# Sampled attention regrouped: one group of plain matrix products per sequence in place of two

## The chip, the cores and the metric

The kernel runs on one core of one Trainium2 chip. The metric is device time in microseconds. A profiled execution gives a trace of each engine: PE is TensorE's matrix product, PEld its weight load, DVE VectorE, ACT ScalarE, POOL GpSimd and SPq the queue of SyncE from which the loads and stores are issued.

## What is computed

One step of a one-layer decoder trunk: a prompt of 1,024 rows and 8 sampled sequences of 8 rows each go through a projection, two branches (a recurrent one, mLSTM, and windowed attention with a sink), a gated merge, an output product and an MLP. The change touches the attention of the sampled sequences alone. Each of them reads its own 128 cached keys and values and the new rows:

```python
def swa_sample(q, k, v, ck, cv, sinks):
    kk = jnp.concatenate([ck.astype(k.dtype), k], axis=1)
    vv = jnp.concatenate([cv.astype(v.dtype), v], axis=1)
    ...
    qh = q.reshape(B, T, A_KV, A_GROUP, A_HD).transpose(0, 2, 3, 1, 4)
    o = sink_attend(qh, kk.transpose(0, 2, 1, 3), vv.transpose(0, 2, 1, 3), mask, sinks)
```

`sink_attend` is a softmax over scaled, masked scores with one more logit per head in the denominator, and then the product with the values.

## The kernel before

Each engine runs a program of its own, in order, and the programs meet at semaphores. The large products (projection, output product, MLP) split each float32 operand into a high and a low part and add three products of the fp32r type. In the projection such a piece of work is a *unit*: 24 products into one bank, of 384 columns (two in three) or 320 columns (one in three), issued by `proj_unit` (line 889). The small products of the attention are plain float32 products and transposes (line 845, by `tr`; lines 1097, 1098 and 1118).

The attention does not run by itself. Lists made at the top of the file (`FILL_P0`, `FILL_SS`, `FILL_P1`, from `spread`) say which units stand between its steps, and `fill` is called with them in every engine's program. `attention()` on PE runs `prompt(0)`, `sampled`, `prompt(1)`. `FILL_SS` has 17 entries: entry 0 holds three units, each of the entries 1 to 16 one. ACT reads each unit (a tanh, line 1451), and DVE applies the gate (lines 2100 to 2104). A unit with number 0 of a block makes SP load the next block of weights (`load_block`, four transfers of 256 KB here, behind a wait for all units of the block two back); in `FILL_SS` these are, besides the first unit, the entries 4, 10 and 16.

For a sampled sequence b the steps are, on PE: `ss_keys(b)` transposes the cached keys (two transposes, waits for their load), `ss_scores(b)` (16 products on 64 x 32 tiles of the array), `ss_transposes(b)` of the probabilities, `ss_values(b)` (16 products with the cached and the new values, on 128 x 32 and 64 x 32 tiles), `ss_outputs(b)` (one transpose of the gathered output). Between them ACT copies (`ss_keys`, `ss_pT`, `ss_out`) and takes exponents (`ss_exps`), and DVE masks (`ss_mask`), divides (`ss_divide`, last line 2038) and gathers (`ss_gather`, line 2050). Cached keys and values have two buffers each. In SP's program `load_keys(s)` waits until the keys of sequence s-2 are transposed (`sk_t`), and `load_values(s)` until the values of sequence s-2 are used (`ss_v`):

```python
if s >= 2:
    sp.wait_ge(sk_t, s - 1)
...
if s >= 2:
    sp.wait_ge(ss_v, s - 1)
```

In the kernel before, PE's round b is: keys of b+1, one unit, outputs of b-1, transposes of b, scores of b+1, one unit, values of b. So each sequence has two groups of plain products between units: (values b-1, keys b+1) and (outputs b-1, transposes b, scores b+1).

After the last round `prompt(1)` begins: scores of its first two heads' units, the last `ss_outputs`, one unit of fill, and `at_transposes`, which waits for DVE's `at_mask` (lines 1991 to 2003) and `at_divide` (line 2011).

Of the kernel before, what the change touches and what calls it, by code (L numbers as in the profile page):

```python
# [38 lines left out]
NSEQ = 8  # L39
# [188 lines left out]
HALF = 2 * NB  # L228
# [18 lines left out]
def layer_kernel(nc, x_prompt, x_sample, state_C, state_n, state_m, cache_k, cache_v, norm_attn, w_in, b_gate,  # L247
# [20 lines left out]
    with ctx:  # L268
# [61 lines left out]
        s = ExitStack()  # L330
# [264 lines left out]
        def _(sp):  # L595
# [154 lines left out]
            def sampled(fills):  # L750
                def load_keys(s):
                    if s >= 2:
                        sp.wait_ge(sk_t, s - 1)
                    sp.dma_start(kc[:, s % 2, :], cache_k[0, s].rearrange("w h d -> w (h d)")).then_inc(kc_in[s % 2], 16)

                def load_values(s):
                    if s >= 2:
                        sp.wait_ge(ss_v, s - 1)
                    sp.dma_start(vc[:, s % 2, :], cache_v[0, s].rearrange("w h d -> w (h d)")).then_inc(vc_in[s % 2], 16)

                sp.wait_ge(at_v, NB)
                sp.wait_ge(at_p1, HALF)
                load_keys(0)
                load_keys(1)
                load_values(0)
                fill(fills[0])
                for s in range(1, NSEQ):
                    fill(fills[2 * s - 1])
                    if s + 1 < NSEQ:
                        load_keys(s + 1)  # L770
                    fill(fills[2 * s])
                    load_values(s)
                fill(fills[2 * NSEQ - 1])
                fill(fills[2 * NSEQ])
                sp.wait_ge(ko_e, 2)
                sp.dma_start(p_k[0, 0].rearrange("t h d -> t (h d)"), kout[:, 0, :]).then_inc(out_dma, 16)
                sp.dma_start(p_v[0, 0].rearrange("t h d -> t (h d)"), avn[:, NT - 2, :]).then_inc(out_dma, 16)
                for s in range(NSEQ):
                    at = slice(s * DSEQ, (s + 1) * DSEQ)
                    sp.dma_start(s_k[0, s, WIN - DSEQ:].rearrange("t h d -> t (h d)"),  # L780
                                 kout[at, 1, :]).then_inc(out_dma, 16)
                    sp.dma_start(s_v[0, s, WIN - DSEQ:].rearrange("t h d -> t (h d)"),
                                 avn[at, NT - 1, :]).then_inc(out_dma, 16)
# [59 lines left out]
        def _(pe):  # L843
# [283 lines left out]
            def prompt(p, fills):  # L1127

                pe.wait_ge(free_a, ATT_FIRST + (ATT_UNITS[0] + ATT_UNITS[1] if p else 0))
                if p:  # L1130
                    pe.wait_ge(ss_te, NSEQ)
                u0 = p * HALF
                at_scores(u0)
                at_scores(u0 + 1)
                if p:
                    ss_outputs(NSEQ - 1)
                fill(fills[0])
                for n in range(0, HALF, 2):
                    u = u0 + n
                    at_transposes(u)  # L1140
                    if n:
                        at_values(u // 2 - 1)
                    if n + 2 < HALF:
                        at_scores(u + 2)
                        at_scores(u + 3)
                    at_transposes(u + 1)
                    fill(fills[n + 1])
                    fill(fills[n + 2])
                at_values(u // 2)

            def sampled(fills):

                for x, i in enumerate((NT - 2, NT - 1)):
                    for p in range(2):
                        last = tr(bank[5 + x][0:rows_of(i), p * P:(p + 1) * P], akT[:, p, cols(i)], P)
                    last.then_inc(ko_t, 1)
                fill(fills[0])
                pe.wait_ge(free_a, FIRST_UNIT[17])
                pe.wait_ge(at_o, NB)
                ss_keys(0)  # L1160
                ss_scores(0)
                pe.wait_ge(ko_e, 2)
                for b in range(NSEQ):
                    if b + 1 < NSEQ:
                        ss_keys(b + 1)
                    fill(fills[2 * b + 1])
                    if b >= 1:
                        ss_outputs(b - 1)
                    ss_transposes(b)
                    if b + 1 < NSEQ:  # L1170
                        ss_scores(b + 1)
                    fill(fills[2 * b + 2])
                    ss_values(b)

            def attention():
                pe.wait_ge(ml_te, 2 * S_PER)
# [196 lines left out]
        def _(act):  # L1373
# [230 lines left out]

            def prompt_act(p, fills):
                u0 = p * HALF
                if p:
                    ss_out(NSEQ - 1)
                at_exps(u0)
                at_exps(u0 + 1)  # L1610
                fill(fills[0])
                for n in range(0, HALF, 2):
                    u = u0 + n
                    at_copy(u)
                    if n:
                        at_out(u // 2 - 1)
                    at_copy(u + 1)
                    if n + 2 < HALF:
                        at_exps(u + 2)
                    fill(fills[n + 1])  # L1620
                    if n + 2 < HALF:
                        at_exps(u + 3)
                    fill(fills[n + 2])
                at_out(u // 2)

            def sampled_act(fills):
                act.wait_ge(ko_t, 2)
                nc.scalar.activation(kout[:, 0, :], bank[5][:, 0:256], ACT.Copy).then_inc(ko_e, 1)
                nc.scalar.activation(kout[0:64, 1, :], bank[6][0:64, 0:256], ACT.Copy).then_inc(ko_e, 1)
                fill(fills[0])  # L1630
                ss_keys(0)
                ss_exps(0)
                for b in range(NSEQ):
                    if b + 1 < NSEQ:
                        ss_keys(b + 1)
                    fill(fills[2 * b + 1])
                    if b >= 1:
                        ss_out(b - 1)
                    ss_pT(b)
                    if b + 1 < NSEQ:  # L1640
                        ss_exps(b + 1)
                    fill(fills[2 * b + 2])


            def square_x(i):
# [136 lines left out]
        def _(dve):  # L1782
# [193 lines left out]
            def at_mask(u):  # L1976
                i, p, gg = at_unit(u)
                dve.wait_ge(at_s, u + 1)
                if u == 0:
                    dve.wait_ge(consts, 5)  # L1980
                if u == HALF:
                    dve.wait_ge(ss_v, NSEQ)
                    dve.wait_ge(ss_ot, NSEQ)
                st = ast[:, u % 2]
                later = amask[:, :].bitcast(I32).unsqueeze(1).broadcast_to([P, 2, P])

                def part(half, kb):
                    return score_bank(u, half)[:, :].rearrange("q (g b k) -> q g b k", g=2, b=2)[:, :, kb, :]
                for half in range(2):
                    prev = part(half, 0) if i else nbig[:, :].unsqueeze(2).broadcast_to([P, 2, P])  # L1990
                    ins = nc.vector.copy_predicated(part(half, 1), later, prev)
                link(ins)
                for half in range(2):
                    ins = nc.vector.tensor_reduce(st[:, 0, 2 * half:2 * half + 2], part(half, 1), mybir.AxisListType.X,
                                                  ALU.max)
                link(ins)
                sk = sink_b[:, :].rearrange("t (v g) -> t v g", g=GRP)[:, 2 * p:2 * p + 2, 2 * gg:2 * gg + 2]

                def by_half(x):
                    return st[:, x, :].rearrange("t (v g) -> t v g", g=2)  # L2000
                link(nc.vector.scalar_tensor_tensor(by_half(1), by_half(0), ATT_SCALE, sk, ALU.mult, ALU.max))
                nc.vector.tensor_scalar(st[:, 2, :], st[:, 1, :], -1.0, None, ALU.mult)
                nc.vector.tensor_tensor(by_half(3), sk, by_half(1), ALU.subtract).then_inc(at_m, 1)
# [48 lines left out]

            def prompt_dve(p, fills):
                u0 = p * HALF
                at_mask(u0)
                at_mask(u0 + 1)
                at_divide(u0)
# [13 lines left out]
            def sampled_dve(fills):  # L2071
# [5 lines left out]
                                                .rearrange("c g (b t) -> c g b t", t=DSEQ))  # L2077
                ins.then_inc(ss_q, 1)
                fill(fills[0])
                ss_mask(0)  # L2080
                ss_divide(0)
                for b in range(NSEQ):
                    fill(fills[2 * b + 1])
                    if b + 1 < NSEQ:
                        ss_mask(b + 1)
                        ss_divide(b + 1)
                    fill(fills[2 * b + 2])
                    ss_gather(b)

            def gated(b, u):  # L2090

# [473 lines left out]
```

## Time and profile before

| | us |
|---|---|
| median of 3 runs | 1671.58 |
| lowest, highest | 1671.13, 1672.65 |
| the profiled execution | 1671.4 |
| its span on the core | 1669.7 |
| PE busy | 1643.3 (98%) |
| DVE busy | 945.5 (57%) |
| ACT busy | 631.3 (38%) |
| POOL busy | 347.9 (21%) |

The time of the profiled execution is its span and 1.7 us around it. A PE line of the timeline gives the start, the time until the last of its products ends, the line and the number of products; since products overlap, the difference between the starts of two lines is the time that the first one takes on the engine. "[0.58 <-ACT kcT L1578]" is idle time before a line and what ended it.

### The profile page before, as it was taken

What the parts mean: (1) busy time and instruction counts of PE and PEld (TensorE: products, weight loads), DVE (VectorE), ACT (ScalarE), POOL (GpSimd) and SP (SyncE); (2) the same over time, 40 slices, a digit from 0 to 9 for tenths busy, and PEclk for the clock granted to TensorE, in tenths of its full rate; (3) what the DMA queues carried; (4) which work ended last, traced back from release to release, by engine and by line L of the source; (5) the groups of instructions that cost most, each with busy time, mean ns of one, the idle gap of its engine ahead of it and who ended that gap; (6) DMA issues with size and microseconds to landing.
All of it is one profiled execution on the core that took longest, in us unless ns stands there. A gap on an engine that the chain in (4) does not pass through costs nothing.

```text
span 1669.7 us, 26868 instructions
## 1 busy us (share of the span) xinstructions
PE 1643.3 (98%) x10083; PEld 1497.1 (90%) x10083; DVE 945.5 (57%) x1745; ACT 631.3 (38%) x1403; POOL 347.9 (21%) x349
## 2 busy tenths in 40 slices
PE   8999999999999999999999999999999999999997
PEld 8999999899998899888978899999999999999996
DVE  5413333443145445763544877777777777766787
ACT  5423333232235423553402443333444443343432
POOL 3002001010001100111000233333333222323354
PEclk9999999999999999999999999999999999999999
DMA  7105354461311132311241111111111111111113
GB/s 219 52 28 135 63 73 87 62 88 27 70 30 26 35 75 45 61 26 26 64 134 50 35 43 51 50 50 50 50 28 48 50 50 50 50 39 37 50 63 114
DMA packets 138795, 99.47 MB, mean 60 GB/s; under 512 B 82377, under 2 KB 128465, under 8 KB 138713
## 3 DMA queue, kind: packets, MB, share of 16 engines
q1 hardware_dynamic: 138712, 98.34, 24.2%
q8 instruction: 56, 0.92, 0.3%
q14 instruction: 27, 0.21, 0.1%
HBM read 88.43 MB, written 11.60 MB: 60 GB/s over the span
## 4 chain that ended last, share of the span: by engine, by line
PE 96%; DVE 2%; DMA 1%; issue 1%; ACT 1%; SPq 0%; POOL 0%; DVEq 0%; POOLq 0%; ACTq 0%
PE bank L889 37%; PE bank L1241 23%; PE bank L1221 6%; PE bank L1274 6%; PE bank L1275 6%; PE bank L1273 6%; PE bank L845 3%; PE bank L1282 2%; PE bank L1074 2%; PE bank L1044 1%; PE bank L946 1%; PE bank L954 1%; PE bank L949 1%; PE bank L991 1%; PE bank L929 0%
## 5 line engine op out<-in xcount | busy, mean ns | idle before, releaser
L1241 PE MATMUL bank<-xT_hi,w_hi 128*128 128x384 f32 (+1 forms) x768 | 250.7, 326 | 1.0 <-DVE xT_lo L1823 1.0
L1241 PE MATMUL bank<-xT_hi,w_lo 128*128 128x384 f32 (+1 forms) x768 | 250.6, 326 | 0.0
L1241 PE MATMUL bank<-xT_lo,w_hi 128*128 128x384 f32 (+1 forms) x768 | 250.5, 326 | 0.0
L889 PE MATMUL bank<-xT_hi,w_hi 128*128 128x384 f32 (+1 forms) x1008 | 193.9, 334 | 0.0
L889 PE MATMUL bank<-xT_hi,w_lo 128*128 128x384 f32 (+1 forms) x1008 | 186.2, 326 | 0.0
L889 PE MATMUL bank<-xT_lo,w_hi 128*128 128x384 f32 (+1 forms) x1008 | 186.1, 326 | 0.0
L889 PEld LDWEIGHTS bank<-xT_hi,w_hi 128*128 128x128 f32 x1008 | 166.7, 188 | 2.7 <-issue 1.0
L889 PEld LDWEIGHTS bank<-xT_lo,w_hi 128*128 128x128 f32 x1008 | 168.8, 188 | 0.0
L2504 POOL TENSOR_TENSOR e<-gain_b,e 128x512 f32<-128x512 f32 x60 | 78.0, 1302 | 435.4 <-ACT gain_b L1752 435.4
L889 PEld LDWEIGHTS bank<-xT_hi,w_lo 128*128 128x128 f32 x1008 | 168.7, 188 | 0.0
L2288 DVE TENSOR_TENSOR x<-bank,x 128x512 f32<-128x512 f32 x210 | 141.9, 689 | 31.6 <-PE bank L1275 30.9
L1798 DVE TENSOR_TENSOR w_lo<-raw,w_hi 128x1024 fp32r<-128x1024 f32 (+1 forms) x54 | 70.4, 1306 | 155.7 <-ACT w_hi L1386 155.7
L1241 PEld LDWEIGHTS bank<-xT_hi,w_hi 128*128 128x128 f32 x768 | 144.2, 188 | 1.8 <-DVE xT_lo L1823 1.1
L1241 PEld LDWEIGHTS bank<-xT_lo,w_hi 128*128 128x128 f32 x768 | 144.2, 188 | 0.6
L1241 PEld LDWEIGHTS bank<-xT_hi,w_lo 128*128 128x128 f32 x768 | 144.2, 188 | 0.0
L1752 ACT ACTIVATE gain_b<-bank 128x512 f32<-128x512 f32 x120 | 71.7, 598 | 147.1 <-PE bank L1275 83.4
L2228 DVE TENSOR_TENSOR hf<-relu 128x384 f32<-128x384 f32 (+1 forms) x96 | 55.8, 581 | 113.7 <-ACT relu L1730 111.3
L1730 ACT ACTIVATE relu<-bank 128x384 f32<-128x384 f32 (+1 forms) x96 | 45.2, 471 | 196.3 <-PE bank L1241 194.4
L1451 ACT ACTIVATE sig<-bank 128x384 f32<-128x384 f32 (+1 forms) x72 | 34.0, 473 | 174.4 <-PE bank L889 174.3
L1273 PE MATMUL bank<-t_hi,a_hi 128*128 128x512 f32 x240 | 93.4, 389 | 1.3 <-issue 1.3
L1274 PE MATMUL bank<-t_hi,a_lo 128*128 128x512 f32 x240 | 94.2, 393 | 0.0
L1275 PE MATMUL bank<-t_lo,a_hi 128*128 128x512 f32 x240 | 94.1, 392 | 0.0
(259 smaller groups left out, 3007.5 us busy)
## 6 DMA issues: line engine op xcount, KB each, us to landing
raw<-in_w_in SPq DMA_DIRECT2D x64, 256.0 KB, 4.6
raw<-in_w_up SPq DMA_DIRECT2D x16, 1024.0 KB, 5.4
raw<-in_w_down SPq DMA_DIRECT2D x16, 1024.0 KB, 5.0
raw<-in_w_in SPq DMA_DIRECT2D x9, 1024.0 KB, 5.7
xin<-in_x_prompt SPq DMA_DIRECT2D x8, 512.0 KB, 4.6
bc<-gate_rows SPq DMA_DIRECT2D x32, 128.0 KB
Cin<-in_state_C SPq DMA_DIRECT2D x4, 1024.0 KB, 7.9
out<-Cin SPq DMA_DIRECT2D x16, 256.0 KB
```

Source lines behind the costliest of these rows:

```text
L845: return nc.tensor.transpose(out, in_, ident[0:rows, 0:rows])
L889: last = nc.tensor.matmul(out, lhsT, rhs, start=(step == 0), stop=(step == 3 * KT - 1))
L1221: last = nc.tensor.matmul(bank[m % out_ring(m)][0:rows_of(i), :], lhsT, w[:, b % 2, g * 512:(g + 1) * 512], start=(step == 0), stop=(step ...
L1241: last = nc.tensor.matmul(bank[unit_bank(g, u)][:, 0:cn], w[:, 0, k * WCOLS + tile * P:k * WCOLS + (tile + 1) * P], x[:, k, c0:c0 + cn], s ...
L1273: nc.tensor.matmul(out[:, :], a_tile(a_hi, a, q), b_part(b, False), start=True, stop=False)
L1274: nc.tensor.matmul(out[:, :], a_tile(a_lo, a, q), b_part(b, False), start=False, stop=False)
L1275: nc.tensor.matmul(out[:, :], a_tile(a_hi, a, q), b_part(b, True), start=False, stop=True).then_inc(gemm_v, 1)
L1752: nc.scalar.activation(gain_b[:, at:at + HD2], bank[PLACE.index(name) % BANKS][:, :], ACT.Copy).then_inc(free_c, 1)
L1798: ins = nc.vector.tensor_tensor(w_lo[:, b % 2, at], raw[:, b % 2, at], w_hi[:, b % 2, at].bitcast(F32), ALU.subtract)
L2228: nc.vector.tensor_tensor(hf[:, tile, c0:c0 + cn], relu[:, u % 2, 0:cn], relu[:, u % 2, 0:cn], ALU.mult).then_inc(sq_done, 1)
L2288: nc.vector.tensor_tensor(v, src, v, ALU.add).then_inc(free_v, 1)
L2504: nc.gpsimd.tensor_tensor(v, gain_b[:, at:at + HD2], v, ALU.add).then_inc(c_added, 1)
```

## The change

SP loads the values of the first two sequences ahead. PE's round b becomes: outputs of b-2, values of b-1, transposes of b, scores of b+1, keys of b+2, and then two units with nothing between them. The first three rounds' lead is set up before the loop: entry 0 of the fills, keys of 0, entry 1, scores of 0, keys of 1, entry 2. Outputs of sequence 6 come right after the last round, and values of sequence 7 move into `prompt(1)`, between its first scores and its first fill, with the outputs of 7 behind that fill. ACT's and DVE's programs follow that order. Two waits at the start of DVE's `at_mask` are dropped, and `prompt_dve(1)` begins with `ss_gather(7)`. In SP's program round s is now `load_values(s+1)` (from s = 1), then `load_keys(s+2)`, then the fills 2s+3 and 2s+4.

```diff
@@ sampled, SP @@
                 load_values(0)
-                fill(fills[0])
-                for s in range(1, NSEQ):
-                    fill(fills[2 * s - 1])
-                    if s + 1 < NSEQ:
-                        load_keys(s + 1)
-                    fill(fills[2 * s])
-                    load_values(s)
-                fill(fills[2 * NSEQ - 1])
-                fill(fills[2 * NSEQ])
+                load_values(1)
+                for n in range(3):
+                    fill(fills[n])
+                for s in range(NSEQ - 1):
+                    if s >= 1:
+                        load_values(s + 1)
+                    if s + 2 < NSEQ:
+                        load_keys(s + 2)
+                    fill(fills[2 * s + 3])
+                    fill(fills[2 * s + 4])
@@ prompt, PE @@
                 if p:
+                    ss_values(NSEQ - 1)
+                fill(fills[0])
+                if p:
                     ss_outputs(NSEQ - 1)
-                fill(fills[0])
@@ sampled, PE @@
                 ss_keys(0)
+                fill(fills[1])
                 ss_scores(0)
+                ss_keys(1)
+                fill(fills[2])
                 pe.wait_ge(ko_e, 2)
                 for b in range(NSEQ):
-                    if b + 1 < NSEQ:
-                        ss_keys(b + 1)
-                    fill(fills[2 * b + 1])
-                    if b >= 1:
-                        ss_outputs(b - 1)
+                    if b >= 2:
+                        ss_outputs(b - 2)
+                    if b >= 1:
+                        ss_values(b - 1)
                     ss_transposes(b)
                     if b + 1 < NSEQ:
                         ss_scores(b + 1)
-                    fill(fills[2 * b + 2])
-                    ss_values(b)
+                    if b + 2 < NSEQ:
+                        ss_keys(b + 2)
+                    if b + 1 < NSEQ:
+                        fill(fills[2 * b + 3])
+                        fill(fills[2 * b + 4])
+                ss_outputs(NSEQ - 2)
@@ prompt_act @@
-                if p:
-                    ss_out(NSEQ - 1)
                 at_exps(u0)
                 at_exps(u0 + 1)
                 fill(fills[0])
+                if p:
+                    ss_out(NSEQ - 1)
@@ sampled_act @@
                 ss_keys(0)
+                fill(fills[1])
+                ss_keys(1)
                 ss_exps(0)
+                fill(fills[2])
                 for b in range(NSEQ):
-                    if b + 1 < NSEQ:
-                        ss_keys(b + 1)
-                    fill(fills[2 * b + 1])
-                    if b >= 1:
-                        ss_out(b - 1)
+                    if b >= 2:
+                        ss_out(b - 2)
                     ss_pT(b)
+                    if b + 2 < NSEQ:
+                        ss_keys(b + 2)
                     if b + 1 < NSEQ:
                         ss_exps(b + 1)
-                    fill(fills[2 * b + 2])
+                        fill(fills[2 * b + 3])
+                        fill(fills[2 * b + 4])
+                ss_out(NSEQ - 2)
@@ at_mask, DVE @@
-                if u == HALF:
-                    dve.wait_ge(ss_v, NSEQ)
-                    dve.wait_ge(ss_ot, NSEQ)
@@ prompt_dve @@
+                if p:
+                    ss_gather(NSEQ - 1)
                 at_mask(u0)
@@ sampled_dve @@
                 fill(fills[0])
+                fill(fills[1])
                 ss_mask(0)
                 ss_divide(0)
+                fill(fills[2])
                 for b in range(NSEQ):
-                    fill(fills[2 * b + 1])
+                    if b >= 1:
+                        ss_gather(b - 1)
                     if b + 1 < NSEQ:
                         ss_mask(b + 1)
                         ss_divide(b + 1)
-                    fill(fills[2 * b + 2])
-                    ss_gather(b)
+                        fill(fills[2 * b + 3])
+                        fill(fills[2 * b + 4])
```

## Rows read from the trace of the kernel before

**Rows 1.** The page: busy time by engine, and granted clock by slice.
```profile
PE 1643.3 (98%) x10083; PEld 1497.1 (90%) x10083; DVE 945.5 (57%) x1745; ACT 631.3 (38%) x1403; POOL 347.9 (21%) x349
...
PEclk9999999999999999999999999999999999999999
```

**Rows 2.** Timeline of PE, one sequence (start us, us, engine, line, what).
```profile
609.55 0.27 PE L845 MATMUL bank<-ident,o 128*128 128x128 f32 x1
609.66 0.38 PE L845 MATMUL bank<-ident,sprob 128*128 128x128 f32 x2
609.97 0.44 PE L1097 MATMUL bank<-kcT,qsmp 64*32 64x128 f32 x8
610.21 0.31 PE L1098 MATMUL bank<-akT,qsmp 64*32 64x64 f32 x8
610.45 1.66 PE L889 MATMUL bank<-xT_hi,w_hi 128*128 128x384 f32 x8
611.95 1.55 PE L889 MATMUL bank<-xT_lo,w_hi 128*128 128x384 f32 x8
613.33 1.55 PE L889 MATMUL bank<-xT_hi,w_lo 128*128 128x384 f32 x8
614.82 0.32 PE L1118 MATMUL bank<-vc,spT 128*32 128x64 f32 x8
615.06 0.32 PE L1118 MATMUL bank<-avn,spT 64*32 64x64 f32 x8
615.31 0.44 PE L845 MATMUL bank<-ident,kc 128*128 128x128 f32 x2
615.50 1.66 PE L889 MATMUL bank<-xT_hi,w_hi 128*128 128x384 f32 x8
617.01 1.55 PE L889 MATMUL bank<-xT_lo,w_hi 128*128 128x384 f32 x8
```

**Rows 3.** Timeline of SP's queue in the same stretch.
```profile
609.74 2.91 SPq L626 DMA_DIRECT2D raw<-in_w_in  x4
...
615.44 0.33 SPq L759 DMA_DIRECT2D vc<-in_cache_v  x1
615.81 0.43 SPq L754 DMA_DIRECT2D kc<-in_cache_k  x1
```

**Rows 4.** Tile kc (cached keys): its eight loads, and their time to landing.
```profile
L754 SPq DMA_DIRECT2D kc<-in_cache_k x8: 328/429/437, 581.9 to 643.3; - x8
...
DMA to landing us min/median/max: 2.0/2.2/3.6
```

**Rows 5.** Timeline of PE where the sampled stage begins.
```profile
594.17 0.38 PE L845 MATMUL bank<-ident,kc 128*128 128x128 f32 x2
595.14 0.45 PE L1097 MATMUL bank<-kcT,qsmp 64*32 64x128 f32 x8 [0.58 <-ACT kcT L1578]
...
595.82 1.66 PE L889 MATMUL bank<-xT_hi,w_hi 128*128 128x384 f32 x8
```

**Rows 6.** Timeline: from one sequence's transposes to the end of its successor's division.
```profile
600.10 0.38 PE L845 MATMUL bank<-ident,sprob 128*128 128x128 f32 x2
...
605.09 0.32 DVE L2038 TENSOR_SCALAR sprob<-sprob,sst 128x192 f32<-128x192 f32 x1
```

**Rows 7.** Timeline of PE and DVE where the prompt's second half begins.
```profile
672.76 0.32 PE L1118 MATMUL bank<-vc,spT 128*32 128x64 f32 x8
...
673.98 0.92 DVE L2050 COPY o<-bank 32x64 f32<-32x64 f32 x4
...
675.43 0.87 DVE L1991 COPY_PREDICATED_SCALAR bank<-amask,nbig 128x256 f32 x2 [0.53 <-PE bank L845]
...
679.91 0.69 DVE L2011 TENSOR_TENSOR prob<-prob,ast 128x512 f32<-128x512 f32 x1
...
680.65 0.66 PE L845 MATMUL bank<-ident,prob 128*128 128x128 f32 x4 [1.18 <-DVE prob L2011]
```

**Rows 8.** PE's longest idle time, and the window around it (granted clock after POOL).
```profile
11.81 1.25 PE L889 MATMUL bank<-w_hi,xT_hi 128*128 128x264 f32 x8 [2.65 <-DVE xT_lo L1823]
```

**Rows 9.** Busy time by window; after POOL the granted clock, DMA share, GB/s.
```profile
10.00:20.00 10.00, 7.31 (x57) 6.79 (x58) 8.80 (x11) 7.07 (x14) 3.25 (x6) 1.00 0.94 303
```

## Prediction

> **What bounds the kernel now.** I read the page first. PE is busy for 98% of the span, at the full granted clock in every slice [rows 1]. So nearly every microsecond that PE waits is one of the result, and what other engines save is worth nothing. The timeline of PE over one sampled sequence then shows what lies between the units [rows 2]. Two groups of plain products stand there. The one at 609.55 takes 0.90 us until the unit begins at 610.45, the one at 614.82 takes 0.68 us until 615.50, and neither has idle time: each step's input comes from a group at least one unit (some 4 us) earlier. Last I read SP's queue [rows 3] and the times to landing [rows 4], since the change reorders that queue too.
>
> **What the group costs beside its own products.** Eight products of 384 columns take 1.38 us (611.95 to 613.33). The first eight behind a group take 1.50 us (610.45 to 611.95) and 1.51 us (615.50 to 617.01), so a return from plain products to fp32r ones costs 0.12 us, whether the group ended in products on 64 x 32 tiles or in whole transposes [rows 2]. The eight ahead of the values take 1.49 us (613.33 to 614.82), 0.11 us more; transposes to scores take 0.31 us for what would be some 0.22 by the 0.11 us of the single transpose ahead of them [rows 2]. Such entries to small tiles number two per sequence, before and after.
>
> The Trainium skill (TensorEngine Tiling, Key Properties) says that changing the tiling mode drains TensorE. The rows on the entries agree. But by that rule the return behind the keys' transposes, which use the same 128 x 128 mode as the units, would be free, and merging groups would save nothing; the row has 0.12 us there. By the rule the sum below would be 0.8 us higher.
>
> **Removed: returns.** Before, there are 16 returns to units: one behind the first keys and scores, one behind each of eight second groups, seven behind values. After, there are 9: keys 0; scores 0 with keys 1; rounds 0 to 6. Seven at 0.12 us are -0.8 us.
>
> **Removed: the wait at the start.** From the first keys' transposes (594.17) to the next unit (595.82) there are 1.65 us, because the scores wait for ACT's copy of the keys [rows 5]. A unit now covers it. What remains is keys 0.19, an entry 0.1, scores 0.48, keys 0.19, or 0.96 us by the spacing of [rows 2]: -0.7 us.
>
> **Added at the start: a wait for the first probabilities.** Transposes of 0 now stand one unit behind scores of 0. In the kernel before, from the end of a unit (600.10) over scores to the end of the division (605.09 + 0.32 = 605.41) there are 5.3 us [rows 6], with a split of weights in the way, as there will be here. PE's group and unit fill 0.9 + 4.2 = 5.1 us. So +0.3 us; queued behind it are round 0 and all that follows. Between later rounds lie two units (7.7 or 8.3 us), which cover this chain with the gather of 0.92 us in front of it [rows 7].
>
> **Added: the wait for the keys.** This is the large term. In SP's new order the load of values s+1 stands ahead of the load of keys s+2. For s of 1 to 5 the values' load waits until PE has done values s-1, and that happens in PE's round s. The same round ends in transposes of keys s+2. So the load of the keys that a round needs at its end is issued only after that round's values product; SP's queue is in order, so it can't pass. Keys 0 to 2 escape this, keys 3 to 7 don't: five waits. Behind PE's wait stand both units of the round, and ACT's copy of the keys with exponents behind it; their users have microseconds to spare.
>
> Its size, counted from the start of the values product: the values' load is issued 0.62 us later (614.82 to 615.44), the keys' load 0.37 us behind it (615.81) [rows 2, 3], and it lands 2.2 us after its issue (median; 2.0 to 3.6) [rows 4], and PE needs some 0.06 us to go on, the same lag as between the end of the values (615.06 + 0.32) and SP's issue. That is 3.25 us. Without a wait the keys' transposes would start after values 0.49, transposes 0.31 and scores 0.48, or 1.28 us [rows 2]. So 1.97 us a round. In rounds 1 and 4 a block of weights was requested one unit (4.2 us) before the group. Such a block takes SP 2.91 us to issue [rows 3], the keys' load follows 5.4 us behind its first issue, and the loads of 3.4 to 3.6 us in this trace were issued 4.1 to 6.1 us behind one, with other loads of keys and values between [rows 4]. I take 2.5 us there, nearer the free value as nothing else is in flight, and keep 3.6 for the range. Sum: 3 x 1.97 + 2 x 2.27 = +10.4 us. Bounds: 5 x 1.77 = 8.9 with 2.0 us to landing, 5 x 3.37 = 16.9 with 3.6 throughout.
>
> **Moved: the end of the stage.** Count from the end of the last unit (672.66, 0.1 us ahead of 672.76). Before, the prompt's first transposes start at 680.65, 8.0 us later: a gather begins at 673.98, the mask at 675.43, and 5.2 us behind that the division ends (679.91 + 0.69) [rows 7]. After, PE does outputs 5, values 6 and transposes 7 (0.9 us) and then stops at outputs 6 for DVE's gather of 6, which can't begin sooner than 1.32 us (the gate of the last unit is ahead of it) and ends at 2.3 us. Then scores of the prompt (1.1 us, ending near 3.6), values 7 (to 4.2), gather 7 (to 5.2), and only then the mask, as DVE now has the gather ahead of it. The transposes follow 5.2 us later, at 10.45 us; the one unit between can't fill that. That is 2.45 us later, but 1.1 us of products that were ahead of the last unit now lie behind it: net +1.35 us. Bounds: nothing, if DVE's and PE's steps overlap better than I lined them up, and 2.45.
>
> The two waits dropped in the mask cost nothing: its own wait for scores and the gather ahead of it cover them. The early load of values 1 is hidden by the three units of entry 0. ACT's output copy of 7 (0.55 us) now stands ahead of its copy of probabilities; PE's scores hide it. No instruction is added or removed.
>
> **The sum.** -0.8 - 0.7 + 0.3 + 10.4 + 1.35 = +10.55 us on the profiled execution's 1671.4, or 1682.0 us. The median of the runs shown is 0.2 above the profiled one, which is within its spread; I keep 1682.0 (+0.6%). After this stage PE is bound by its own products to the end, so nothing gives the delay back.
>
> **Rivals.**
> *The keys are there in time.* If the keys' load reached the chip before the scores end, the five waits would vanish and the rest gives -0.8 - 0.7 + 0.3 + 1.35, or 1671.6: not slower. The place is the keys' transposes of rounds 1 to 5. It decides from a time to landing under 0.3 us (3.25 less 2.2, against 1.28), or if SP's order were not binding. The shortest of eight loads took 2.0 us [rows 4], and the order follows from semaphores that can't be met sooner. If the end of the stage costs nothing too, it is 1670.2, still within 0.2%; a gain needs returns dearer than rows show. 5%.
>
> *Every load meets traffic.* With 3.5 us to landing throughout (values' load just ahead on the same queue, as at 615.81), three rounds gain 1.3 and two 1.0: +5.9, or 1687.9. Against it: that load's values and keys were the third and fourth in flight behind a block; after, at most a block's tail and one load precede. 7%.
>
> *The clock falls in the waits.* PE would stand for 2 us every 10. If the granted clock fell from 2.4 to 1.2 GHz and one unit (4.2 us) after each wait ran at half the rate, it costs 5 x 4.2 = 21 us: 1703. Against it: PE idled 2.65 us before 11.81 [rows 8], and the clock in that window stayed 1.00, the level of 2.4 GHz [rows 9]. 3%. The Trainium skill (TensorE: Matmul & The Clock Gate, HAM oscillation) warns of just this, waits for a transfer that put a warmed TensorE back to half rate in each round of a loop; by it this rival would be the forecast, while the row has the clock stay full through 2.65 us.
>
> *The merge is worth nothing* (returns are free): +0.8, 1682.8, inside the range.
>
> **How the numbers follow.** The forecast has 85%, the rivals 5, 7 and 3. Low end: landing in 2.0 us (-1.5) and a free end of the stage (-1.35) with a little more, 1678.5. High end: the two rounds behind a block at 3.5 (+2.0), free returns (+0.8), the end at 2.45 (+1.1), 1686.0. The rivals at 1671.6, 1687.9 and 1703 stay outside, with 15% and some tails. A measurement of this kernel can tell about 0.2%, 3.3 us, from no change. Slower takes the forecast and two rivals less a little: 0.94. Within 0.2%: 0.04, the first rival's most. Faster: 0.02.
>
> **What would show it.** In the timeline of PE after: five lines of keys' transposes with idle time near 2.0 us ended by the transfer of kc, and none at the keys of 0 to 2; SP issuing kc 0.37 us behind vc each time, 0.6 us behind the start of a values product; one group between pairs of units, with 0.12 us in the first eight products; no 0.58 us wait at the first scores; a wait of some 1.3 us at outputs 6 and of some 1.7 us at the prompt's first transposes; a granted clock of 1.00 throughout. No wait on kc would make the prediction wrong, and so would a clock of 0.5 in this stretch, or a saving beside the waits of over 2 us.

## The result and the profile after

| | before | after |
|---|---|---|
| median, us | 1671.62 | 1688.18 |
| lowest to highest, us (4 runs each) | 1671.13 to 1672.65 | 1685.85 to 1688.52 |
| ratio, 95% interval | | 1.0096 [1.0083, 1.0108] |
| the profiled execution, us | 1671.4 | 1688.24 |
| its span, us | 1669.7 | 1686.5 |
| PE busy, us | 1643.3 | 1649.5 |

The change makes the kernel 16.6 us slower (medians), where 10.4 (1682.0 less 1671.62) were forecast: 1688.18 lies above the range's 1686.0. The page of after, in the lines that answer to [rows 1]:

```profile
PE 1649.5 (98%) x10083; PEld 1503.4 (89%) x10083; DVE 946.3 (56%) x1745; ACT 630.5 (37%) x1403; POOL 346.3 (21%) x349
...
PEclk9999999999999998999999999999999999999999
```

PE has the same 10,083 products and is busy for 6.2 us more, and one slice of the granted clock is an 8. Waiting alone would not raise the busy time. So there are two effects, one of waiting and one of pace. (Of the 6.2 us, 5.4 arise in the sampled stage, as shown below, and 0.75 between 10 and 20 us, in a window to which the part on the clock comes back.) The timeline of PE after, rounds 1 to 3, answers to [rows 2] (start, time, engine, line, product, idle time before it and its releaser):

```profile
613.15 0.32 PE L1119 MATMUL bank<-vc,spT 128*32 128x64 f32 x8
613.40 0.32 PE L1119 MATMUL bank<-avn,spT 64*32 64x64 f32 x8
613.65 0.44 PE L846 MATMUL bank<-ident,sprob 128*128 128x128 f32 x2
614.02 0.44 PE L1098 MATMUL bank<-kcT,qsmp 64*32 64x128 f32 x8
614.26 0.31 PE L1099 MATMUL bank<-akT,qsmp 64*32 64x64 f32 x8
616.56 0.44 PE L846 MATMUL bank<-ident,kc 128*128 128x128 f32 x2 [1.99 <-DMA kc<-in_cache_k]
616.75 2.40 PE L890 MATMUL bank<-xT_hi,w_hi 128*128 128x384 f32 x8
618.95 2.40 PE L890 MATMUL bank<-xT_lo,w_hi 128*128 128x384 f32 x8
621.19 1.55 PE L890 MATMUL bank<-xT_hi,w_lo 128*128 128x384 f32 x8
622.58 1.33 PE L890 MATMUL bank<-xT_hi,w_hi 128*128 128x320 f32 x8
...
629.51 0.44 PE L846 MATMUL bank<-ident,kc 128*128 128x128 f32 x2 [1.79 <-DMA kc<-in_cache_k]
629.70 1.65 PE L890 MATMUL bank<-xT_hi,w_hi 128*128 128x384 f32 x8
...
633.97 1.55 PE L890 MATMUL bank<-xT_hi,w_hi 128*128 128x384 f32 x8
...
643.16 0.69 PE L846 MATMUL bank<-ident,kc 128*128 128x128 f32 x2 [3.41 <-DMA kc<-in_cache_k]
643.50 2.48 PE L890 MATMUL bank<-xT_hi,w_hi 128*128 128x320 f32 x8
645.78 2.33 PE L890 MATMUL bank<-xT_lo,w_hi 128*128 128x320 f32 x8
```

In each of the rounds 1 to 5 PE stops at the keys' transposes for the load of kc: 1.99, 1.79, 3.41, 1.90 and 1.80 us, 10.89 us in sum. Behind the second wait a unit of 384 columns takes 4.27 us (629.70 to 633.97). Behind the first the same kind takes 5.83 us (616.75 to 622.58), and its first eight products 2.20 us (616.75 to 618.95). The windows over these stretches show the granted clock (after the x counts of POOL), then DMA share and GB/s:

```profile
610.00:620.00 10.00, 8.01 (x67) 7.22 (x66) 3.69 (x18) 1.83 (x7) 0.00 (x0) 0.87 0.68 131
640.00:650.00 10.00, 6.84 (x31) 6.84 (x32) 3.61 (x17) 1.99 (x9) 0.00 (x0) 0.66 0.10 27
655.00:665.00 10.00, 8.12 (x41) 8.12 (x42) 3.50 (x18) 1.40 (x5) 0.00 (x0) 0.83 0.12 32
```

These windows average over stretches at 2.4 GHz (1.00) and at 1.2 GHz (0.50). A window that lies inside the slow unit of round 3 has the lower level alone:

```profile
643.50:647.00 3.50, 3.50 (x15) 3.50 (x14) 0.64 (x3) 0.91 (x4) 0.00 (x0) 0.50 0.00 0
```

The units behind the waits of rounds 1, 3 and 4 take 1.56, 2.05 and 1.57 us longer than their like at the full clock. In round 3 the keys' transposes take 0.15 us longer too, and the second unit 0.03. Together that is 5.36 us.

SP's queue after answers to [rows 3]; the first two columns are the start of an issue and its duration:

```profile
609.09 2.88 SPq L626 DMA_DIRECT2D raw<-in_w_in  x4
613.78 0.34 SPq L759 DMA_DIRECT2D vc<-in_cache_v  x1
614.16 0.43 SPq L754 DMA_DIRECT2D kc<-in_cache_k  x1
626.92 0.33 SPq L759 DMA_DIRECT2D vc<-in_cache_v  x1
627.29 0.43 SPq L754 DMA_DIRECT2D kc<-in_cache_k  x1
638.96 0.33 SPq L759 DMA_DIRECT2D vc<-in_cache_v  x1
639.33 0.43 SPq L754 DMA_DIRECT2D kc<-in_cache_k  x1
```

The values' load is issued 0.63 us behind the start of the values product (613.15 to 613.78), the keys' load 0.38 us behind that. The order and both distances are as forecast (0.62 and 0.37).

### The profile page after: what moved, and what is told of

Same layout as the page of the kernel before. It is cut to its first block, busy times and chain, and to the rows that moved or that the text cites. A ratio compares the mean times of both kernels' runs of the same rounds, so it can differ in the third digit from the quotient of the medians.

```text
span 1686.5 us, 26868 instructions
## 1 busy us (share of the span) xinstructions
PE 1649.5 (98%) x10083; PEld 1503.4 (89%) x10083; DVE 946.3 (56%) x1745; ACT 630.5 (37%) x1403; POOL 346.3 (21%) x349
## 4 chain that ended last, share of the span: by engine, by line
PE 95%; DVE 2%; DMA 1%; issue 1%; ACT 1%; SPq 0%; POOL 0%; DVEq 0%; POOLq 0%; ACTq 0%
PE bank L890 37%; PE bank L1250 23%; PE bank L1230 6%; PE bank L1283 6%; PE bank L1284 6%; PE bank L1282 6%; PE bank L846 3%; PE bank L1291 2%; PE bank L1075 2%; PE bank L1045 1%; PE bank L955 1%; PE bank L947 1%; DMA kc<-in_cache_k 1%; PE bank L950 1%; PE bank L992 1%
```

## The experiments

Ten kernels ran: the changed kernel once more, and nine that alter one thing in it or one more thing in one of the nine. "Ratio" is to the kernel before, with its 95% interval. Where the sampled stage alone is compared, its length is counted in the profiled execution, from the first keys' transposes to the prompt's first transposes. It is 86.48 us before and 103.52 us in the changed kernel.

### 1. Keys' load ahead of values' load

```diff
-                    if s >= 1:
-                        load_values(s + 1)
                     if s + 2 < NSEQ:
                         load_keys(s + 2)
+                    if s >= 1:
+                        load_values(s + 1)
```

> The changed kernel with one thing altered: in SP's rounds the load of keys s+2 stands ahead of the load of values s+1. Theory A (the delay is the keys' load queued behind the values' load, five waits of 1.8 to 3.4 us, 10.9 us in sum, and 5.3 us in which units behind three of these waits ran at a lower granted clock because PE had idled): both go, no wait on kc, granted clock 1.00 through the stage, 1688.2 - 16.2 = 1672.0 us. Rival B (the clock fell because of the new grouping or of the traffic, not because of the idle time): the waits go, the clock still falls in some rounds, 1677 us. Rival C (the waits move to another load, values or weights): over 1680 us.

Measured: 1676.37 us, ratio 1.0029 [1.0019, 1.0039]. Three of the five waits are gone; two stay, in rounds 1 and 4. The timeline of PE has them, and SP's shows why (kernel e1_keys_first):

```profile
615.77 0.44 PE L846 MATMUL bank<-ident,kc 128*128 128x128 f32 x2 [1.44 <-DMA kc<-in_cache_k]
...
646.59 0.44 PE L846 MATMUL bank<-ident,kc 128*128 128x128 f32 x2 [1.52 <-DMA kc<-in_cache_k]
646.78 2.40 PE L890 MATMUL bank<-xT_hi,w_hi 128*128 128x384 f32 x8
648.97 2.40 PE L890 MATMUL bank<-xT_lo,w_hi 128*128 128x384 f32 x8
```

```profile
608.82 2.71 SPq L626 DMA_DIRECT2D raw<-in_w_in  x4
611.57 1.14 SPq L754 DMA_DIRECT2D kc<-in_cache_k  x1
```

In those rounds the keys' load still stands behind a block of weights, which waits for a unit of the round before and is issued only when that unit is done; the keys then landed 4.2 us after their issue, in both rounds. My 1672.0 missed that. One of the two waits, that of 1.52 us, again has a slow unit behind it (1.54 us). Against the changed kernel's profiled run, the waits are 7.93 us shorter and the slow units 3.82 us; the time fell by 11.87.

### 2. The same with the old end of the stage

Between round 7 and outputs 6 stands a unit again, values 7 follow these at once, and the prompt's second half begins as before the change. PE's part of it, to which ACT and DVE are fitted:

```diff
                     if b + 1 < NSEQ:
                         fill(fills[2 * b + 3])
+                    if b + 2 < NSEQ:
                         fill(fills[2 * b + 4])
+                fill(fills[2 * NSEQ])
                 ss_outputs(NSEQ - 2)
+                ss_values(NSEQ - 1)
```

> The kernel of e1_keys_first with the end of the stage put back: a unit stands between round 7 and outputs 6, values 7 come right behind these, and the prompt's second half begins as in the kernel before. Theory: the new end costs 1.35 us net, and one return to units more costs 0.12; transposes 7 now stand one unit behind scores 7 and may wait 0.4 us for the division. 1672.0 - 0.9 = 1671.1 us. If the new end was free: 1672.3 us.

Measured: 1675.45 us, ratio 1.0023 [1.0013, 1.0032]: 0.92 us less than experiment 1, where 0.9 were expected. The intervals overlap, so the size is not shown. The two waits are 1.53 and 1.49 us here. The first has slow work behind it (transposes 0.15 and unit 1.38 us), the second has none, the other way round than in experiment 1. As both kernels carry these waits, whose after-effects vary, experiments 6 and 7 repeat the pair without them.

### 3. PE busy while it waits

```diff
             def ss_keys(b):
+                if b >= 3:
+                    pe.wait_ge(sk_e, b)
+                    for x in range(8):
+                        nc.tensor.matmul(bank[3][:, 0:P], ident[:, :], ident[:, :], start=True, stop=True)
                 pe.wait_ge(kc_in[b % 2], 16 * (b // 2 + 1))
```

> The changed kernel with eight idle products (identity by identity, 128 columns, plain float32) ahead of the keys' transposes of sequences 3 to 7, about 1.7 us of work that PE does while it would wait for the keys' load; nothing else differs. Theory A (the clock fell because PE idled): waits on kc shrink to 0.1 to 0.3 us, PE reaches the units at the same time as before, the granted clock stays 1.00, and the 5.3 us of slow units go: 1683 us. Rival B (traffic or grouping lowers the clock): 1688 us, clock below 1 in some rounds. If the added products are not hidden: over 1690 us.

Measured: 1682.88 us, ratio 1.007 [1.0053, 1.0087], 5.3 us under the changed kernel and 0.1 from what theory A gave. In round 1 (timeline of PE, e3_busy_in_wait):

```profile
614.39 2.05 PE L1084 MATMUL bank<-ident 128*128 128x128 f32 x16
616.29 0.44 PE L846 MATMUL bank<-ident,kc 128*128 128x128 f32 x2
616.48 1.66 PE L890 MATMUL bank<-xT_hi,w_hi 128*128 128x384 f32 x8
617.97 1.55 PE L890 MATMUL bank<-xT_lo,w_hi 128*128 128x384 f32 x8
```

(The trace counts each of these plain products of full size twice.) The keys' transposes start 1.9 us late as before, but the unit runs at 1.49 us for its first eight products. The same windows as above:

```profile
610.00:620.00 10.00, 10.00 (x90) 9.24 (x90) 3.58 (x18) 1.83 (x7) 0.00 (x0) 1.00 0.66 133
640.00:650.00 10.00, 10.00 (x91) 9.29 (x90) 3.68 (x18) 2.82 (x12) 0.00 (x0) 1.00 0.62 116
655.00:665.00 10.00, 10.00 (x95) 9.29 (x94) 3.63 (x16) 2.43 (x11) 0.00 (x0) 1.00 0.09 28
```

The clock is full in all three windows, and every unit of the stage takes its usual time, although the loads and the grouping of the products are the same. The DMA share in these windows is no guide either: the clock is 1.00 at 0.62 and 0.66 here and was 0.66 at 0.10 in the changed kernel. So it is PE's idle time that lowers the clock, and traffic and grouping are out. Only in round 4 did PE still idle, for 1.17 us, as the load landed late there (3.5 us); the clock stayed. Useless work in the wait bought 5.3 us.

### 4. A longer wait

```diff
+                    if s >= 1 and s + 2 < NSEQ:
+                        sp.wait_ge(vc_in[(s + 1) % 2], 16 * ((s + 1) // 2 + 1))
                     if s + 2 < NSEQ:
                         load_keys(s + 2)
```

> The changed kernel with a longer wait: SP issues the load of keys s+2 only when values s+1 have landed, so each of the five waits grows by some 1.9 us, from about 2.0 to 3.9 us. Theory A (idle time lowers the clock, and a longer wait does so more surely): 5 x 1.9 = 9.5 us of waiting more and slow units behind all five waits in place of three, some 4 us more: about 1702 us. Rival B (the clock does not depend on the wait): 1697 or 1698 us, with slow units behind three waits or fewer.

Measured: 1698.57 us, ratio 1.0162 [1.0145, 1.0178]. The waits are 3.38, 3.21, 4.10, 3.52 and 3.12 us, 17.33 in sum: 6.44 more than in the changed kernel, not 9.5, since a keys' load that had followed the values' load on the queue now travels alone (1.9 or 2.0 us to landing, where it had 2.2 to 3.8). Slow units follow all five (2.39, 1.56, 2.10, 1.37, 1.07 us), and four of the five pairs of transposes are 0.15 us slow: 9.1 us, 3.7 more. 6.4 and 3.7 make 10.1; the profiled runs differ by 10.2.

### 5. A shorter wait

```diff
                     if s >= 1:
-                        load_values(s + 1)
+                        sp.wait_ge(ss_v, s)
                     if s + 2 < NSEQ:
                         load_keys(s + 2)
+                    if s >= 1:
+                        load_values(s + 1)
```

> The changed kernel with each of the five waits shortened by the 0.37 us of one issue: SP still waits for values s-1, but then issues the load of keys s+2 first and the load of values s+1 behind it. Theory A (waiting and the idle time's effect on the clock): waits of about 1.6 us, 5 x 0.37 = 1.85 us less, and slow units behind some of them still, as e1_keys_first had one behind a wait of 1.52 us: 1684 to 1686.5 us. Rival (the clock stays full below some 1.8 us of idle time): 1681 us and a clock of 1.00 in the stage.

Measured: 1679.95 us, ratio 1.0057 [1.0041, 1.0074]; one of four runs took 1684.24. The waits are 1.40, 1.26, 1.34, 1.65 and 1.30 us, 6.95 in sum, and in this profile the clock is full behind each. Theory A's number fell and the rival's came out. The time is 8.2 us under the changed kernel; in the stage the profile has 3.9 us less idle time and the 5.4 us of slow work gone. It is no clean bound, though: waits of 1.52 and 1.53 us in experiments 1 and 2 did lower the clock, and waits of 1.79 and 1.80 us in the changed kernel did not. The run of 1684.24 has the lowest mean clock of the four (0.994, where the others have 0.995 to 0.997), so a slow unit there is likely, but that run has no trace.

### 6 to 9. Nothing waits for keys any more

Experiment 6 issues each keys' load a round earlier, ahead of the round's values and weights:

```diff
+                load_keys(2)
                 for s in range(NSEQ - 1):
+                    if s + 3 < NSEQ:
+                        load_keys(s + 3)
                     if s >= 1:
                         load_values(s + 1)
-                    if s + 2 < NSEQ:
-                        load_keys(s + 2)
```

> The changed kernel with the keys' loads taken out of the way of both other queues: load of keys 2 ahead of SP's loop, and in round s the load of keys s+3 (free as soon as keys s+1 are transposed) ahead of values s+1 and of the fills with their weight blocks. In e1_keys_first two waits were left (1.44 and 1.52 us, rounds 1 and 4, behind a block of weights) and one of them lowered the clock. Theory: no wait on kc and a granted clock of 1.00 in the whole stage; what is left of the change is -0.8 (returns) -0.7 (start) +0.3 (first division) +1.35 (end) = +0.15 on the kernel before: 1671.7 us. Rival (the regrouping itself costs time that no wait shows): 1674 us or more.

Measured: 1672.74 us, ratio 1.0003 [0.9994, 1.0012]. No wait on kc is left, and the clock is 1.00 in the whole stage. From the changed kernel's profiled 1688.24, less 10.89 of waits and 5.36 of slow units, one gets 1671.99; this profiled run took 1672.08. That this is within 0.1 us is in part luck, as single executions of this kernel lie 1.6 us apart. The stage alone took 86.95 us, 16.57 less than in the changed kernel. Waits and slow units make 16.25 of these. The rest is a cost that every wait has beside its idle time: without one, the keys' transposes start 0.24 us behind the start of the last scores (614.53 to 614.77, experiment 6), with one the idle time begins only when these have ended, 0.31 us behind it. Five times 0.07 is 0.35 us.

Experiment 7 is 6 with the end of experiment 2:

> e6_keys_early with the end of the stage put back as in e2_keys_first_old_end: -1.35 for the end, +0.12 for one return, +0.4 for the wait of transposes 7 on their division (0.38 us in e2): 1670.9 us. If the new end costs nothing, 1672.2.

Measured: 1671.49 us, ratio 0.9996 [0.9987, 1.0005], 1.25 us under experiment 6, where 0.8 were expected (medians of 11 runs each; the two intervals overlap). The stage took 86.27 us, 0.68 less than in experiment 6, and experiments 1 and 2 also differ by 0.68 there (91.60 and 90.92). With the return (0.12) and the wait of transposes 7 (0.38) that the old end adds, the new end costs 1.2 us net, against the 1.35 of the forecast.

Experiment 8 is 6 with the keys' transposes in a group of their own between the two units of a round, which adds six returns:

```diff
+                    if b + 1 < NSEQ:
+                        fill(fills[2 * b + 3])
                     if b + 2 < NSEQ:
                         ss_keys(b + 2)
                     if b + 1 < NSEQ:
-                        fill(fills[2 * b + 3])
                         fill(fills[2 * b + 4])
```

> e6_keys_early with the keys' transposes of sequences 2 to 7 in a group of their own, between the two units of a round: six returns from plain products to fp32r ones more, same work. By the rows' 0.12 us for a return, +0.7 us on e6_keys_early: 1672.4; the trace should show 1.50 us in place of 1.38 for the first eight products behind each of the six. If only a change of tile mode cost time (these transposes use the units' mode), +0.0.

Measured: 1672.56 us, ratio 1.0005 [0.9996, 1.0014], or 0.2 less than experiment 6, not 0.7 more. Medians can't tell so little; the stage in the profile can: 87.25 us, 0.30 more than experiment 6. Its timeline tells why it is not 0.7:

```profile
618.19 1.55 PE L891 MATMUL bank<-xT_hi,w_lo 128*128 128x384 f32 x8
619.58 0.38 PE L847 MATMUL bank<-ident,kc 128*128 128x128 f32 x2
619.72 1.42 PE L891 MATMUL bank<-xT_hi,w_hi 128*128 128x320 f32 x8
620.98 1.34 PE L891 MATMUL bank<-xT_lo,w_hi 128*128 128x320 f32 x8
622.15 1.33 PE L891 MATMUL bank<-xT_hi,w_lo 128*128 128x320 f32 x8
```

The return is there (620.98 less 619.72 is 1.26 us, against the 1.17 from 620.98 to 622.15: 0.09 us). But the two transposes behind a unit take 0.14 us (619.58 to 619.72), where behind scores they take 0.19. Six times the difference is some 0.3 us. So a return saved by merging is half given back inside the group.

Experiment 9 is 7 with outputs 7 behind the prompt's first unit and the mask's two waits dropped:

```diff
-                if p:
-                    ss_outputs(NSEQ - 1)
                 fill(fills[0])
+                if p:
+                    ss_outputs(NSEQ - 1)
```

> e7_keys_early_old_end with the outputs of sequence 7 (and ACT's copy of them) behind the prompt's first unit, and without the mask's two waits on the sampled stage, as the change had it. PE's wait of 0.44 us for the last gather goes, and the mask starts some 0.5 us earlier, so the prompt's first transposes too: -0.5 us, 1670.4 us; the best of these kernels and 0.07% below the kernel before, less than a measurement of this kernel tells. If the mask is bound elsewhere, 1670.9.

Measured: 1671.0 us, ratio 0.9996 [0.9987, 1.0005]. The wait of 0.44 us for the gather is gone and the one at the prompt's first transposes is 1.06 us. It is the fastest here, but by its runs it can't be told from the kernel before. Its stage took 85.63 us, 0.85 less than before, in one profile of each.

### 10. The changed kernel again

> The changed kernel as it is, once more, to see how much of its time varies: five waits on kc again, each 1.8 to 2.0 us except where a load lands late; if the late one (3.41 us in round 3, landing 3.8 us after issue, with a transfer of instructions in the same stretch) belongs to the program's place it is again in round 3 or near it, and if it is chance it is elsewhere or missing. Lower clock behind two to four of the waits. 1686 to 1689 us.

Measured: 1688.09 us, ratio 1.0097 [1.008, 1.0114]. The five waits are 1.92, 1.70, 3.13, 1.83 and 1.75 us. The long one is in round 3 again. Slow units follow rounds 1, 3 and 5 this time, not 1, 3 and 4. In two profiles the late load stands in the same place of the program; which of the short waits lowers the clock does not.

## Why the prediction was right or wrong

**The keys' waits: right.** Five waits, their place and their cause came out as told, 10.9 us against 10.4 in idle time, and 0.35 more that I had not counted, as each wait also ends the overlap with the scores (experiment 6). The rounds behind a weight block were cheaper than taken (1.99 and 1.90, not 2.27). Round 3 was dearer: its load took 3.8 us to land, in a stretch where I had priced 2.2. The first rival, keys in time, fell. So did the second, traffic for every load: its 1687.9 is almost the time measured, but that is chance, as four of the five loads landed in 2.2 to 2.4 us and not in 3.5.

**The clock: wrong, and the cause of the miss.** The step that failed is the one that put the clock's term at nothing: that it stays at 1.00 through waits of 2 us, with the third rival at 3% and outside the range. It happened in part: three of five waits had slow units behind them, 5.4 us in sum, where the rival was priced as all five with 4.2 us each (1703). Experiment 3 shows the idle time to be the cause. I had set it aside on one wait of 2.65 us and one window with the clock at 1.00 [rows 8, 9]. But that was one execution. The same wait and the same window in the changed kernel's profile (this code is untouched by the change):

```profile
11.94 1.25 PE L890 MATMUL bank<-w_hi,xT_hi 128*128 128x264 f32 x8 [2.75 <-DVE xT_lo L1836]
...
10.00:20.00 10.00, 8.06 (x54) 8.06 (x55) 7.70 (x9) 7.08 (x14) 3.10 (x6) 0.83 0.95 304
```

Of the twelve profiles of this study, ten have a clock below 1.00 in that window, behind a wait of 2.5 to 3.0 us; the row I read was one of the two exceptions. A single row in which the clock stayed showed that it can stay, not that it does. In hindsight, with a chance of a half for each wait (four of the eight short ones in two profiles of the changed kernel) and 1.6 us per slow unit (rounds 1 and 4), the term is +4 us and the forecast 1686.

The Trainium skill (TensorE: Matmul & The Clock Gate, HAM oscillation) warned of loops whose waits for a transfer put TensorE back to half rate, and I weighed that against the row. The direction of its warning holds here, at 0.66 to 0.87 in the windows above. I read too much into it when I wrote that by it the rival would be the forecast: its rule of thumb names idle gaps longer than the 2 us that I expected. As a bound that rule is too lenient here, as a gap of 1.52 us was enough.

**The returns: mis-sized.** I took -0.8 us, seven times 0.12. Inside the merged group the transposes now stand behind values and take 0.37 us (613.65 to 614.02 above), where behind outputs they took 0.31 [rows 2]. A round with two 384 column units takes 10.17 us in experiment 6 against 10.23 before: 0.06 us a round, so -0.4 us. The Trainium skill's rule that a change of tiling mode drains TensorE (TensorEngine Tiling, Key Properties) fits this give-back, as the number of such changes is the same in both orders; no run separates the two. The return has a price of its own beside it: 0.09 to 0.12 us even behind whole transposes, where that rule gives none. The fourth rival, a merge that is worth nothing, was half true: 0.4 of the 0.8 us came.

**The start: right.** The wait for the first probabilities is there, 0.26 us against 0.3, and the 0.58 us at the first scores are gone.

**The end: right in mechanism.** Timeline of PE and DVE after, at the end of the stage; it answers to [rows 7]:

```profile
688.99 0.92 DVE L2060 COPY o<-bank 32x64 f32<-32x64 f32 x4
689.96 0.33 PE L846 MATMUL bank<-ident,o 128*128 128x128 f32 x1 [1.03 <-DVE o L2060]
...
691.88 0.92 DVE L2060 COPY o<-bank 32x64 f32<-32x64 f32 x4 [1.98 <-PE bank L1119]
692.73 0.85 DVE L2001 COPY_PREDICATED_SCALAR bank<-amask,nbig 128x256 f32 x2
...
697.95 0.66 PE L846 MATMUL bank<-ident,prob 128*128 128x128 f32 x4 [1.66 <-DVE prob L2021]
```

From the last unit's end (687.79) to the prompt's transposes there are 10.2 us, against 10.45 worked out, with waits of 1.03 and 1.66 us (1.3 and 1.7). Gather, then mask, then 5.2 us is the chain that was named. Its net price of 1.35 us was 1.2 by the profiles of experiments 6 and 7, as worked out there.

**The sum again.** From the stage's beginning (594.17 and 594.43) to the prompt's transposes (680.65 and 697.95) the changed kernel needs 17.0 us more: 10.9 waits for keys, 5.4 clock, and +0.8 for all the rest, where my terms for the rest gave +0.15. Of that 0.6 us, 0.4 are the returns and 0.35 the lost overlap at the five waits; the end was some 0.15 us cheaper than taken. What is left is under 0.1 us.

## What to carry to other kernels

When a consumer's order is regrouped, walk the loading queue with it: a load must not stand behind one that waits for a later step of the same round. Here the repair is a matter of a few lines and takes back 15.4 us, after which the regrouping is worth nothing that the runs can tell. Price a wait on TensorE of over some 1.5 us at its length plus the slow unit that may follow (1.1 to 2.5 us each here), and before calling the clock safe on the strength of a row look at the same wait in more than one profile. If a wait can't be removed, idle products in it keep the clock (5.3 us here).

## What the runs showed of the hardware

- Whether idle time of TensorE lowers the granted clock is not settled by its length alone. Behind the waits of 1.26 to 1.65 us in experiment 5's profile it never fell, and behind those of 1.64 to 1.66 us at the prompt's first transposes it fell in none of eight profiles. Of the two waits in experiment 1 it fell behind that of 1.52 us and not behind that of 1.44, in experiment 2 behind that of 1.53 and not behind that of 1.49. Behind those of 1.7 to 2.0 us in the changed kernel it fell in four of eight cases in two profiles, and behind those of 3.1 to 4.1 us in seven of seven. What else decides was not tested.
- The slowest eight products of 384 columns in a row took 2.71 us (experiment 2, 616.60 to 619.31), where their like take 1.50 us. A whole unit never took twice its time (at most 6.66 us against 4.27 for 384 columns in experiment 4, and 6.10 against 3.62 for 320 in experiment 10). The unit behind it was at most 0.04 us slow.
- The awaited keys' loads of 128 KB landed 1.9 to 2.0 us after their issue where they were issued alone (experiment 4), 2.1 to 2.4 us right behind the values' load, and 4.2 us right behind a block of weights (experiment 1). The late ones (3.8 and 3.5 us, round 3 of the changed kernel in both profiles) fall together with a transfer of instructions. The DMA view of that stretch, and below it that of round 2, which has none:

```profile
q1 hardware_dynamic: 288, 0.26, 15.9%
q8 instruction: 1, 0.02, 1.4%
...
kc<-in_cache_k SPq DMA_DIRECT2D x1, 128.0 KB, 3.8
```

```profile
q1 hardware_dynamic: 288, 0.26, 23.0%
...
kc<-in_cache_k SPq DMA_DIRECT2D x1, 128.0 KB, 2.2
```

  Three more profiles fit: the load in flight beside such a transfer landed late in experiment 3 (round 4, keys 3.5 and values 3.6 us, with a block of weights just ahead), in experiment 4 (round 3, values 2.9, the keys issued behind it 2.0) and in experiment 5 (round 3, values 3.5, the keys issued ahead of them 2.1). That the one delays the other is likely but was not tested.
